# A hybrid encoder block on one core: the order of the last two experts' products on TensorE

## The chip, the cores and the metric

One core of one Trainium2 chip runs the whole block in one launch, in f32. The metric is the device time of a run in microseconds (us), of which the median of several runs counts. Engines are called as in the profile: PE is TensorE (PEld its weight load), DVE is VectorE, ACT is ScalarE, POOL is GpSimd, SP is SyncE, which here only issues transfers.

## What is computed

For 512 tokens of width 1024, one layer:

```
u = RMSNorm(h);  h += concat(pool mixer(u W_in), bidirectional SSM(u W_in)) W_out
v = RMSNorm(h)
every token picks 1 of 4 expert groups and in it 2 of 8 experts (32 experts in all)
h += sum over its two experts of  weight * (silu(v Wg) * (v Wu)) Wd        Wg, Wu: 1024x256, Wd: 256x1024
h += sigmoid(RMSNorm(h) W_g + b_g) * (p W_ple)
out = RMSNorm(h)
```

The change touches the third and fourth line, from the last two experts to the first transposes for the product with `W_g`.

## The kernel before, in words

**Experts.** The tokens of an expert are gathered into 64 places (`CAP`); should an expert have more tokens, overflow rounds run afterwards, inside an `If` on every engine, which is not taken with these inputs. Experts are numbered 0 to 31 (`NE` is 32). For expert e PE runs four steps. `gu_step(e)` is the gate and up product: 16 matmuls of 64 tokens by 256 columns into bank `1 + e % 2`, gate in its lower and up in its upper 64 partitions. ACT's `silu(e)` and DVE's `hidden` turn it into the hidden rows. `h_step(e)` transposes those on PE into bank 3, DVE copies them out, and `down_step(e)` is the down product: 4 matmuls of 512 columns into bank `4 + e % 2`. ACT's `y_out(e)` copies it to the buffer `M_Y + e % 3` and counts `dn_sb` up. For experts 0 to 29 POOL then scatters these rows to a table of pairs (token, first or second expert) in HBM. A matmul of f32 has two records in the trace.

**Order on PE.** The order is written out by hand in the loop over e at line 1988: `h_step(e)`, for some e the transposes of gathered rows (`x_step`), `gu_step(e + 1)`, for some e other small work (`p_rows`, `proj`), and `down_step(e)`. So the next expert's gate and up product covers what ACT and DVE do for this one. ACT has the matching order at line 779: `silu(e + 1)` ahead of `y_out(e)`.

**Weights.** Each expert has three pieces of 1 MB, 96 MB in all, loaded by SP into 22 or so places that are freed by earlier products. SP issues transfers in order, and behind the last piece it issues, each after its wait: the residual `h` back from HBM (2 MB), the first half of half 0 of `W_g` (`load_gate(0, 0, 4)`, 1 MB, when expert 30's gate and up product is done), then `pairs` of token tile 0 (1 MB, when POOL reports `moe_done`, which is after the last scattered rows have been stored, and when expert 30's down product is done), the rest of half 0 (1 MB), then (when expert 31's gate and up product is done) pairs of tile 1, half 1 of `W_g` (2 MB), pairs of tile 2, and pairs of tile 3.

**Combining.** The 512 tokens are 4 tiles (t) of 128. DVE's `combine(t)` first waits for the pairs of tile t, adds the two weighted rows to `h` (4 operations of 512 columns, L1332), and then adds what experts 30 and 31 contribute, which is in PSUM (2 operations, L856, which count the semaphore `comb`). That contribution is not scattered: PE spreads it over the tokens by `combined(t)` at line 1915. For each half n of the columns it has two matmuls, one for expert 30 and one for expert 31, each with a 64 row contraction (n = 0 on the lower 64 rows, n = 1 on the upper ones) into bank `2 * t + n`: 16 spreading products in all. They stand behind `down_step(31)`, the `If`, and a wait for all 32 copies `dn_sb`. Then comes `turned_h(t)` (8 transposes of the new `h` into banks 2t and 2t + 1, each four behind a wait on `comb`), DVE writes the transposed tile to `ut`, and `gate(2 * t)`, `gate(2 * t + 1)` are the products with `W_g` (8 matmuls of 512 columns each). The order is `turned_h(0)`, `gate(0)`, `turned_h(1)`, `gate(1)`, `gate(2)`, and so on:

```
            for t in range(NT):
                combined(t)
            ...
            turned_h(0)
            pe.wait_ge(ld_wple, 32)
            for t in range(NT):
                gate(2 * t)
                if t + 1 < NT:
                    turned_h(t + 1)
                pe.wait_ge(ld_wple1, 16)
                gate(2 * t + 1)
```

PE executes its list in order, so a wait holds up all that stands behind it. All matmuls go through a helper at L1580, whence this line in the profile; L1948 is the transpose of `h_step`, L2044 that of `turned_h`, L754 is `silu`, L531 ACT's copy, L1569 POOL's `moe_done`, L488 and L494 are SP's loads of `W_g` and of the pairs.

## Time and profile before

| | us |
|---|---|
| median of 3 runs | 523.2 (522.0 to 524.99) |
| the profiled execution, its own time | 525.58 |
| its span, first to last instruction | 523.7 |
| PE busy / DVE / ACT / POOL | 482.2 / 239.0 / 163.2 / 159.9 |
| granted PE clock, mean over the span | 0.982 of full speed |
| HBM read / written | 138.17 MB / 16.29 MB |

The profiled execution's own time is 1.9 us above its span; what a step moves is looked for in the span. A row of a timeline gives the start, the length, the engine and line, output and inputs, the count of records, and in brackets the idle time before it with what ended it. In windows the granted clock is a share of full speed (1.00 is 2.4 GHz, 0.50 is 1.2 GHz).

### The profile page before, as it was taken

How to read it: one execution, taken by the hardware profiler on the slowest of the kernel's cores; microseconds unless marked ns; L12 is line 12 of the kernel's file. 1: busy time of each engine (PE TensorE's matmuls, PEld its weight loads, DVE VectorE, ACT ScalarE, POOL GpSimd, SP SyncE). 2: the span in 40 equal slices, each digit the busy share in tenths (PEclk: the TensorE clock that was granted, in tenths of full speed). 3: DMA queues.
4: the chain of work that ended last, by engine and by line, in shares of the span. 5: the costliest groups of instructions: out<-in, count | busy, mean ns of one | idle time of the engine just before them, and what ended most of it. 6: DMA issues, size and time to landing. Idle time of an engine off the chain costs nothing.

```text
span 523.7 us, 7297 instructions
## 1 busy us (share of the span) xinstructions
PE 482.2 (92%) x2744; PEld 271.8 (52%) x2744; DVE 239.0 (46%) x683; ACT 163.2 (31%) x265; POOL 159.9 (31%) x144
## 2 busy tenths in 40 slices
PE   3799999999999998979999999879999998899993
PEld 3446776634844477645555555435454544444441
DVE  2899987999233358632222222202211211474524
ACT  5643335456442344111111111112211121314464
POOL 1069999944100111222222232202120210003350
PEclk9999999999999999979999999989999998999997
DMA  8874200499289966998999999999999997970012
GB/s 295 145 201 88 62 0 2 159 131 212 103 370 419 402 252 259 397 417 334 419 420 417 419 416 414 418 419 421 420 420 418 418 417 299 340 314 0 0 80 80
DMA packets 57083, 146.83 MB, mean 280 GB/s; under 512 B 27602, under 2 KB 32758, under 8 KB 44248
## 3 DMA queue, kind: packets, MB, share of 16 engines
q1 hardware_dynamic: 50872, 133.92, 69.0%
q0 software_dynamic: 5904, 12.41, 6.1%
q8 instruction: 22, 0.36, 0.3%
q14 instruction: 13, 0.11, 0.1%
q10 hardware_dynamic: 272, 0.04, 0.0%
HBM read 138.17 MB, written 16.29 MB: 295 GB/s over the span
## 4 chain that ended last, share of the span: by engine, by line
PE 70%; DMA 20%; ACT 4%; DVE 4%; issue 1%; SPq 0%; DVEq 0%; POOL 0%; POOLq 0%
PE bank L1580 64%; DMA big<-in_exp_w_up_dram 6%; DMA ring<-in_exp_w_up_dram 6%; DMA h<-in_exp_w_up_dram 5%; DMA moe<-v_d,gidx_all 2%; PE bank L1929 2%; DMA h<-in_x_dram 1%; PE bank L1671 1%; ACT moe L531 1%; PE bank L1948 1%; ACT L539 1%; DVE moe L856 1%; PE bank L1815 1%; PE bank L2044 1%; DVE ring L856 1%
## 5 line engine op out<-in xcount | busy, mean ns | idle before, releaser
L1580 PE MATMUL bank<-ring,moe 128*64 128x256 f32 (+3 forms) x976 | 130.1, 392 | 3.8 <-DMA ring<-in_exp_w_up_dram 3.8
L1580 PEld LDWEIGHTS bank<-ring,moe 128*64 128x64 f32 (+1 forms) x976 | 76.9, 147 | 40.7 <-issue 17.4
L1506 POOL DMA_INDIRECT pairs_d<-moe,sidx_all x32 | 31.9, 998 | 163.1 <-PE bank L1929 84.0
L856 DVE TENSOR_TENSOR vrow<-moe,bank 64x128 f32<-64x128 f32 x64 | 18.6, 291 | 125.2 <-ACT moe L754 124.2
L1580 PE MATMUL bank<-ut,big 128*128 128x512 f32 x128 | 57.4, 596 | 2.4 <-ACT ut L543 2.4
L1580 PE MATMUL bank<-big,ut 128*128 128x512 f32 x128 | 56.6, 595 | 1.1 <-ACT ut L676 1.1
L754 ACT ACTIVATE moe<-bank 64x256 f32<-64x256 f32 x32 | 12.1, 377 | 145.9 <-PE bank L1580 145.9
L1580 PE MATMUL bank<-ring,ut 128*128 128x512 f32 x128 | 55.7, 593 | 0.4 <-DVE ut L856 0.4
L531 ACT ACTIVATE moe<-bank 128x512 f32<-128x512 f32 x56 | 32.5, 598 | 62.2 <-PE bank L1580 49.5
L1580 PE MATMUL bank<-big,moe 128*64 128x256 f32 (+1 forms) x264 | 43.5, 443 | 5.3 <-DMA zbuf<-in_exp_w_up_dram 2.5
L856 DVE TENSOR_TENSOR ring<-ring,bank 128x64 f32<-128x64 f32 (+1 forms) x142 | 39.5, 278 | 2.8
L1580 PEld LDWEIGHTS bank<-big,ut 128*128 128x128 f32 x128 | 23.9, 190 | 31.0 <-issue 30.7
L1580 PEld LDWEIGHTS bank<-ring,ut 128*128 128x128 f32 x128 | 24.0, 190 | 29.3 <-issue 29.3
L1580 PEld LDWEIGHTS bank<-ut,big 128*128 128x128 f32 x128 | 23.4, 190 | 27.8 <-issue 27.2
L856 DVE TENSOR_TENSOR bank<-bank,ring 128x64 f32<-128x64 f32 (+1 forms) x142 | 35.2, 287 | 2.9
L1580 PE MATMUL bank<-ring 128*64 128x128 f32 (+1 forms) x128 | 32.5, 437 | 0.0
L1580 PEld LDWEIGHTS bank<-big,moe 128*64 128x64 f32 x264 | 22.0, 142 | 20.1 <-issue 6.4
L1269 DVE COPY moe<-bank 128x128 f32<-128x128 f32 x32 | 9.3, 292 | 45.6 <-PE bank L1948 45.6
L856 DVE TENSOR_TENSOR moe<-bank,vec 128x512 f32<-128x512 f32 x40 | 26.0, 687 | 7.7 <-PE bank L1929 5.7
L1580 PEld LDWEIGHTS bank<-ring 128*64 128x64 f32 (+1 forms) x128 | 15.2, 163 | 15.3 <-issue 15.0
L1574 POOL TENSOR_TENSOR ring<-ring,zbuf 128x512 f32<-128x512 f32 x6 | 8.1, 1350 | 48.3 <-ACT ring L817 48.3
L531 ACT ACTIVATE zbuf<-bank 128x512 f32<-128x512 f32 x16 | 11.5, 717 | 35.9 <-PE bank L1580 35.9
(193 smaller groups left out, 605.0 us busy)
## 6 DMA issues: line engine op xcount, KB each, us to landing
ring<-in_exp_w_up_dram SPq DMA_DIRECT2D x19, 1024.0 KB, 22.8
ring<-in_exp_w_down_dram SPq DMA_DIRECT2D x18, 1024.0 KB, 27.9
ring<-in_exp_w_gate_dram SPq DMA_DIRECT2D x17, 1024.0 KB, 23.3
big<-in_exp_w_gate_dram SPq DMA_DIRECT2D x7, 1024.0 KB, 25.5
big<-in_exp_w_down_dram SPq DMA_DIRECT2D x7, 1024.0 KB, 30.0
big<-in_exp_w_up_dram SPq DMA_DIRECT2D x6, 1024.0 KB, 31.4
ut<-in_exp_w_gate_dram SPq DMA_DIRECT2D x4, 1024.0 KB, 12.8
h<-in_exp_w_up_dram SPq DMA_DIRECT2D x4, 1024.0 KB
```

The costliest lines, as they stand in the source:

```text
L531: act.activation(o, i, ACT.Copy).then_inc(signal, 1)
L539: act.activation(at(small, ALL, S_WARM + k, [[1, 1]]), at(small, ALL, S_EPS, [[1, 1]]), function)
L754: act.activation(at(moe, (0, CAP), M_SG, [[1, DE]]), at(bank[1 + e % 2], (0, CAP), 0, [[1, DE]]), ACT.Silu).then_inc(sg_sb, 1)
L856: return dve.tensor_tensor(o, a, b, op)
L1269: dve.tensor_copy(at(moe, ALL, M_HT + (e % 2) * P, [[1, P]]), bank[3][:, 0:P]).then_inc(hT_sb, 1)
L1506: pool.indirect_dma_start(pairs, bass.IndirectOffsetOnAxis(ap=index, axis=0), at(moe, ALL, M_Y + k * 512, [[1, 512]]), None, bounds_check= ...
L1574: seq(pool.tensor_tensor(sg, sg, at(zbuf, ALL, n * 512, [[1, 512]]), ALU.mult))
L1580: return pe.matmul(o, a, b, start=start, stop=stop, skip_group_check=loose)
L1671: last = pe.transpose(bank[B_WT + ri][:, (g % 4) * P:(g % 4 + 1) * P], rv(R_W + ri * 1024 + g * P, P), ident)
L1815: rows = pe.transpose(bank[H_BANK[t] + n][:, (j % 4) * P:(j % 4 + 1) * P], at(h, ALL, t * DM + j * P, [[1, P]]), ident)
L1929: last = pe.transpose(bank[j // 4 * 6][:, (j % 4) * P:(j % 4 + 1) * P], at(moe, ALL, M_XG + k * DM + j * P, [[1, P]]), ident)
L1948: return pe.transpose(bank[3][:, 0:P], vrow[:, :], ident)
```

## The change

Expert 30's down product is moved ahead of expert 31's gate and up product (and on ACT `y_out(30)` ahead of `silu(31)`). Its eight spreading products are taken out of `combined` and put at several places: tile 0 both halves and tile 3 half 0 behind expert 31's gate and up product, tile 3 half 1 behind expert 31's transpose, tile 1 both halves and tile 2 half 0 behind the `If` and ahead of the wait for expert 31's copy, tile 2 half 1 still inside `combined(2)`. `combined(t)` keeps expert 31's products. `turned_h(0)` now stands between `combined(1)` and `combined(2)`. Overflow rounds, which do not run with these inputs, use banks 2, 5 and 3 in place of 0, 6 and 1, since the spread sums are already standing in the others, and PE waits for all copies ahead of them.

```diff
--- before.py
+++ after.py
@@ -777,7 +777,7 @@
 
             silu(0)
             for e in range(NE):
-                if e + 1 < NE:
+                if e < NE - 2:
                     silu(e + 1)
                 if e == P_ROWS:
                     p_rows_out()
@@ -789,6 +789,8 @@
                 y_out(e)
                 if e == 0:
                     slots_30_out()
+                if e == NE - 2:
+                    silu(e + 1)
             with act.If(most(act) > CAP):
                 act.wait_ge(dn_sb, NE)
                 with act.Fori(1, ROUNDS) as r:
@@ -796,7 +798,7 @@
                         turn = act.snap((r - 1) * NE + e + 1)
                         count = act.snap(turn + NE)
                         act.wait_ge(gu_ps, count)
-                        act.activation(at(moe, (0, CAP), M_SG, [[1, DE]]), at(bank[1], (0, CAP), 0, [[1, DE]]),
+                        act.activation(at(moe, (0, CAP), M_SG, [[1, DE]]), at(bank[3], (0, CAP), 0, [[1, DE]]),
                                        ACT.Silu).then_inc(sg_sb, 1)
                         act.wait_ge(dn_ps, count)
                         copy(at(moe, ALL, M_Y + O_Y * 512, [[1, 512]]), bank[4][:, :], dn_sb)
@@ -1218,12 +1220,12 @@
             peak(qv("r1", [[1, 2 * NT]]), qv("pa", [[NE, 2 * NT], [1, NE]]), ALU.add)
             own.do(dve.tensor_reduce(at(flag, ALL, 0, [[1, 1]]), at(bank[5], ALL, NT * NE, [[1, NE]]), AX.X, ALU.max))
 
-            def x_out(k, signal, rows=0):
+            def x_out(k, signal, rows=0, banks=(0, 6)):
 
                 for n in range(2):
                     if rows:
                         dve.wait_ge(xT_ps, rows - 1 + n)
-                    tt(at(moe, ALL, M_XT + k * DM + n * 512, [[P, 4], [1, P]]), at(bank[n * 6], ALL, 0, [[P, 4], [1, P]]),
+                    tt(at(moe, ALL, M_XT + k * DM + n * 512, [[P, 4], [1, P]]), at(bank[banks[n]], ALL, 0, [[P, 4], [1, P]]),
                        at(vec, ALL, V_FFN + 4 * n, [[1, 4], [0, P]]), ALU.mult).then_inc(signal, 1)
 
             x_out(0, xT_sb, 2)
@@ -1314,9 +1316,9 @@
                         tokens(at(gidx_o, ALL, 0, [[1, 1]]), at(tblw, ALL, e, [[1, 1]]), o_idx)
                         half_rows(at(sidx_o, ALL, 0, [[1, 1]]), at(tblw, ALL, e, [[1, 1]]), o_idx)
                         dve.wait_ge(xT_ps, rows_count)
-                        x_out(0, xT_sb)
+                        x_out(0, xT_sb, 0, (2, 5))
                         dve.wait_ge(sg_sb, count)
-                        hidden(bank[1], hg_sb)
+                        hidden(bank[3], hg_sb)
                         dve.wait_ge(hT_ps, count)
                         dve.tensor_copy(at(moe, ALL, M_HT, [[1, P]]), bank[3][:, 0:P]).then_inc(hT_sb, 1)
             with dve.Else():
@@ -1912,21 +1914,25 @@
                     got = pe.transpose(bank[7 if x == NE - 1 else 6][:, t * P:(t + 1) * P], at(moe, ALL, Q[f"X{x}"] + t * P, [[1, P]]), ident)
                 got.then_inc(ppt_ps, 1)
 
+            def spread(x, t, n):
+
+                parts = (n * CAP, (n + 1) * CAP)
+                turned = (at(ring, parts, E_S + t * P, [[1, P]]) if x == NE - 1 else
+                          at(small, parts, S_S30 + t * P, [[1, P]]) if t < 2 else at(rw, parts, (t - 2) * P, [[1, P]]))
+                return mm(bank[2 * t + n][:, :], turned, at(moe, parts, M_Y + x % YBUF * 512, [[1, 512]]),
+                          x == NE - 2, x == NE - 1, True)
+
             def combined(t):
 
                 for n in range(2):
-                    parts = (n * CAP, (n + 1) * CAP)
-                    for x in (NE - 2, NE - 1):
-                        turned = (at(ring, parts, E_S + t * P, [[1, P]]) if x == NE - 1 else
-                                  at(small, parts, S_S30 + t * P, [[1, P]]) if t < 2 else at(rw, parts, (t - 2) * P, [[1, P]]))
-                        got = mm(bank[2 * t + n][:, :], turned, at(moe, parts, M_Y + x % YBUF * 512, [[1, 512]]),
-                                 x == NE - 2, x == NE - 1, True)
-                    got.then_inc(cmb_ps, 1)
-
-
-            def x_rows(k):
+                    if (t, n) == (2, 1):
+                        spread(NE - 2, t, n)
+                    spread(NE - 1, t, n).then_inc(cmb_ps, 1)
+
+
+            def x_rows(k, banks=(0, 6)):
                 for j in range(KC):
-                    last = pe.transpose(bank[j // 4 * 6][:, (j % 4) * P:(j % 4 + 1) * P],
+                    last = pe.transpose(bank[banks[j // 4]][:, (j % 4) * P:(j % 4 + 1) * P],
                                         at(moe, ALL, M_XG + k * DM + j * P, [[1, P]]), ident)
                     if j % 4 == 3:
                         last.then_inc(xT_ps, 1)
@@ -1985,7 +1991,7 @@
             slots(NE - 2)
             pe.wait_ge(ppt_sb, 2)
             x_step(1)
-            for e in range(1, NE):
+            for e in range(1, NE - 2):
                 h_step(e)
                 if e % 2 == 0 and e + 2 < NE:
                     if e == P_ROWS + 1:
@@ -1993,16 +1999,27 @@
                     if e - 1 in P_PROJ:
                         pe.wait_ge(pp_done, 2 * P_PROJ.index(e - 1) + 2)
                     x_step(e // 2 + 1)
-                if e + 1 < NE:
-                    gu_step(e + 1)
+                gu_step(e + 1)
                 if e == P_ROWS:
                     p_rows()
                 if e in P_PROJ:
                     for n in range(2):
                         proj(e, 2 * P_PROJ.index(e) + n)
                 down_step(e)
+            h_step(NE - 2)
+            down_step(NE - 2)
+            gu_step(NE - 1)
+            pe.wait_ge(ppt_sb, 5)
+            pe.wait_ge(dn_sb, NE - 1)
+            spread(NE - 2, 0, 0)
+            spread(NE - 2, 0, 1)
+            spread(NE - 2, 3, 0)
+            h_step(NE - 1)
+            spread(NE - 2, 3, 1)
+            down_step(NE - 1)
             pe.wait_ge(slot_done, 1)
             with pe.If(most(pe) > CAP):
+                pe.wait_ge(dn_sb, NE)
                 with pe.Fori(1, ROUNDS) as r:
                     with pe.Fori(0, NE) as e:
                         turn = pe.snap((r - 1) * NE + e + 1)
@@ -2012,10 +2029,10 @@
                         dma16 = pe.snap(turn * 16)
                         dma48 = pe.snap(turn * 48)
                         pe.wait_ge(o_xg, dma16)
-                        x_rows(0)
+                        x_rows(0, (2, 5))
                         pe.wait_ge(xT_sb, x_count)
                         pe.wait_ge(o_w, dma48)
-                        gate_up(0, 0, (ring, O_SLOT), (ring, O_SLOT + PIECE), 1).then_inc(gu_ps, 1)
+                        gate_up(0, 0, (ring, O_SLOT), (ring, O_SLOT + PIECE), 3).then_inc(gu_ps, 1)
                         pe.wait_ge(hg_sb, h_count)
                         h_rows().then_inc(hT_ps, 1)
                         pe.wait_ge(hT_sb, count)
@@ -2024,10 +2041,10 @@
             with pe.Else():
                 pass
 
-            pe.wait_ge(ppt_sb, 5)
+            for n in (0, 1):
+                spread(NE - 2, 1, n)
+            spread(NE - 2, 2, 0)
             pe.wait_ge(dn_sb, NE)
-            for t in range(NT):
-                combined(t)
             def gate(n):
                 t, half = n // 2, n % 2
                 for j in range(KC):
@@ -2045,7 +2062,11 @@
                                             at(h, ALL, t * DM + j * P, [[1, P]]), ident)
                     last.then_inc(turned_ps, 1)
 
+            combined(0)
+            combined(1)
             turned_h(0)
+            combined(2)
+            combined(3)
             pe.wait_ge(ld_wple, 32)
             for t in range(NT):
                 gate(2 * t)
```

## Rows read from the trace of the kernel before

**Rows 1.** The page's chain of work that ended last, by engine.

```profile
PE 70%; DMA 20%; ACT 4%; DVE 4%; issue 1%; SPq 0%; DVEq 0%; POOL 0%; POOLq 0%
```

**Rows 2.** The chain in order of time (start us, us, what), the wait for the last weights.

```profile
407.18 31.39 DMA big<-in_exp_w_up_dram
```

**Rows 3.** PE timeline, 430 to 465 us: start us, us, operation [idle before <-releaser].

```profile
430.59 5.39 PE L1580 MATMUL bank<-ring,moe 128*64 128x256 f32 x40 [0.96 <-DMA ring<-in_exp_w_up_dram]
435.92 0.33 PE L1948 MATMUL bank<-cst,vrow 128*128 128x128 f32 x1
438.62 7.08 PE L1580 MATMUL bank<-big,moe 128*64 128x256 f32 x40 [2.38 <-DMA big<-in_exp_w_up_dram]
...
446.34 1.94 PE L1580 MATMUL bank<-big,moe 128*64 128x512 f32 x8 [0.38 <-DVE moe L1269]
449.07 1.14 PE L1580 MATMUL bank<-moe,small 64*128 64x512 f32 x4 [0.79 <-ACT moe L531]
...
456.21 1.09 PE L2044 MATMUL bank<-cst,h 128*128 128x128 f32 x8
457.74 7.11 PE L1580 MATMUL bank<-ring,ut 128*128 128x512 f32 x16 [0.44 <-DVE ut L856]
```

**Rows 4.** Windows around the last expert: busy us per engine, PEclk, DMA share, GB/s.

```profile
436.30:438.62 2.32, 0.00 (x0) 0.00 (x1) 0.27 (x1) 0.33 (x1) 0.98 (x1) 1.00 1.03 407
438.62:446.34 7.72, 7.34 (x41) 3.69 (x41) 0.87 (x3) 0.97 (x2) 0.09 (x1) 0.78 0.48 189
...
449.07:456.21 7.14, 7.14 (x32) 4.00 (x32) 4.21 (x6) 1.82 (x3) 0.00 (x0) 1.00 1.01 399
```

**Rows 5.** Two stretches of 2 us from 228 us on, same columns.

```profile
228.00:230.00 2.00, 0.91 (x5) 0.50 (x7) 1.26 (x4) 0.00 (x0) 1.70 (x2) 0.57 0.99 406
...
232.00:234.00 2.00, 2.00 (x12) 1.13 (x10) 0.00 (x0) 0.00 (x0) 0.00 (x0) 0.50 1.02 422
```

**Rows 6.** PE timeline, 334 to 352 us: two more waits for weights.

```profile
338.34 0.43 PE L1580 MATMUL bank<-big,moe 128*64 128x256 f32 x1 [2.53 <-DMA zbuf<-in_exp_w_up_dram]
...
347.66 4.71 PE L1580 MATMUL bank<-h,moe 128*64 128x256 f32 x26 [3.67 <-DMA h<-in_exp_w_up_dram]
```

**Rows 7.** The 2 us right behind the second of those waits, columns as in Rows 4.

```profile
348.00:350.00 2.00, 2.00 (x12) 1.17 (x10) 0.00 (x0) 0.00 (x0) 0.00 (x0) 0.50 0.97 403
```

**Rows 8.** ACT timeline around the last expert.

```profile
444.03 0.38 ACT L754 ACTIVATE moe<-bank 64x256 f32<-64x256 f32 x1 [7.40 <-PE bank L1580]
...
448.33 0.60 ACT L531 ACTIVATE moe<-bank 128x512 f32<-128x512 f32 x1 [1.99 <-PE bank L1580]
```

**Rows 9.** DVE timeline, 444 to 458 us.

```profile
444.44 0.61 DVE L856 TENSOR_TENSOR vrow<-moe,bank 64x128 f32<-64x128 f32 x2 [7.87 <-ACT moe L754]
...
451.46 2.99 DVE L1332 SCALAR_TENSOR_TENSOR h<-big,small,h 128x512 f32<-128x512 f32 x4 [5.17 <-DMA big<-pairs_d]
454.55 1.29 DVE L856 TENSOR_TENSOR h<-bank,h 128x512 f32<-128x512 f32 x2
456.90 1.29 DVE L856 TENSOR_TENSOR ut<-bank,vec 128x512 f32<-128x512 f32 x2 [1.07 <-PE bank L2044]
```

**Rows 10.** POOL timeline: the step behind the last stored rows.

```profile
444.23 0.09 POOL L1569 MEMSET fill<- 1x1 int32 x1 [5.85 <-issue]
```

**Rows 11.** SP timeline: issues of the gate weights' first half and of the pairs.

```profile
434.31 0.38 SPq L488 DMA_DIRECT2D ring<-in_ple_gate_w_dram  x1
445.79 0.34 SPq L494 DMA_DIRECT2D big<-pairs_d  x1
446.17 0.43 SPq L488 DMA_DIRECT2D ring<-in_ple_gate_w_dram  x1
```

**Rows 12.** DMA issues of 434 to 435 us: the last column is us to landing.

```profile
ring<-in_ple_gate_w_dram SPq DMA_DIRECT2D x1, 1024.0 KB, 14.6
```

**Rows 13.** DMA issues of 446.1 to 446.3 us and the one before them, us to landing.

```profile
big<-pairs_d SPq DMA_DIRECT2D x1, 1024.0 KB, 5.6
ring<-in_ple_gate_w_dram SPq DMA_DIRECT2D x1, 1024.0 KB, 8.5
```

## The prediction

> **What bounds the kernel now.** I read the chain first: PE holds 70% of the span, DMA 20% [rows 1]. In order of time, PE has to wait for the up weights of expert 31, which land at 438.6 [rows 2], and from there every piece up to the tail is PE's: the change lies on the path that sets the end. The reader should then walk PE's timeline from 435.9 us on [rows 3]: the transpose of expert 30, an idle 2.38 us for the weights, 7.08 us for 40 records (32 of expert 31's gate and up product, 8 of expert 30's down product), an idle 0.38, 1.94 for expert 31's down product, an idle 0.79, the spreading products from 449.07, the first transposes of the new h at 456.21, an idle 0.44, and from 457.74 the products with W_g, which run on to the tail. These four idle times, 4.0 us together, are what the change can fill. The start of gate(0), 457.74, is the point to watch: all behind it is untouched and stays PE's, so the time moves by what this start moves.
>
> Next look at who else arrives at that point. DVE begins tile 0 at 451.46, as the pairs of tile 0 land, after 5.17 us of waiting; four operations take 2.99, and the two that add the spread sums 1.29, from 454.55 to 455.84 [rows 9]. PE comes to the transposes only 0.4 us later, at 456.21 [rows 3]. So PE and the chain DMA, DVE, PE are nearly level at this point, and shortening one of them alone gives little. That is the main reading.
>
> **What ends the wait for the pairs.** SP issues them at 445.79 [rows 11], right after expert 30's down product, and they land 5.6 us later, at 451.4 [rows 13]. Ahead of them in SP's list stands 1 MB of W_g, issued at 434.31 [rows 11] and landing 14.6 us later, at 448.9 [rows 12]. Behind them stands the next 1 MB, issued at 446.17 and landing 8.5 us later, at 454.7 [rows 11, 13]. Landings 2.5 and 3.3 us apart fit transfers of 1 MB passing one after the other: at the 399 GB/s of the busy stretch 1 MB takes 2.6 us [rows 4]. Yet between 438.62 and 446.34 the mean DMA share is only 0.48 [rows 4]: most of the 16 engines have finished, and the slowest still work on the earlier pieces. I conclude that a landing is set by the slowest engine, which has a backlog until 448.9, and that pairs issued at any time before that land at 451.4. The Trainium skill (DMA: Bandwidth & Descriptors, Queues, rings and completion order) says that each engine takes its descriptors in the order of its ring; by that rule too a short new transfer waits behind the backlog, and the spacing above agrees.
>
> **The change, part by part.**
>
> 1. Expert 30's down product moves into the wait for the weights. Its weights stand ahead of expert 31's in SP's list. The transpose ends at 436.25, DVE's copy takes as long as the same step at expert 31, where PE idled 0.38, and the product takes 1.94 [rows 3]: 436.6 to 438.5, so it fits before 438.6. It no longer stands behind the gate and up product: 8 records, a good 1.7 us (1.94 less the last one's tail), are off PE.
>
> 2. With this wait filled, the clock should not fall there. Between 438.62 and 446.34 it was 0.78 of full speed on the mean, after 2.32 us without a matmul [rows 4]. At full clock such 40 records take 5.4 us (the same mixture starting at 430.59 did [rows 3]), so the fall cost 7.08 - 5.4 = 1.7.
>
> 3. What used to be hidden behind expert 30's down product now has no such cover: silu begins as the gate and up product ends and takes 0.38, DVE's two operations 0.61 with 0.03 between [rows 8, 9]; with hand-overs 1.35 us from the end of the product to the next transpose. Three spreading products take the cover's place. 16 of them take 7.14 us, 0.45 each, with two on different halves of the rows side by side [rows 4]; a lone one takes up to twice that. So tile 0's two take 0.9 and tile 3's one 0.45 to 0.9: 1.7 us for 1.35 of cover. Another lone one, up to 0.9, stands ahead of expert 31's down product for an idle 0.38; three more, 1.7, stand where 0.79 was idle [rows 3]. The If's register load may show there: 0 to 0.79, since all of it lay inside that idle time before.
>
> 4. The sum on PE. Gate and up 438.6 to 442.3 (32 records of the full-clock rate, 3.7), spreads to 444.0, transpose 0.3, spread to 445.2, down product to 446.9, three spreads to 448.6, expert 31's on tile 0 and tile 1, two times 0.86, to 450.3. Before, PE had all 16 done at 456.2. Six microseconds early, it now stands at `turned_h(0)`.
>
> 5. Other queues. ACT copies expert 30's rows at 438.5, ahead of silu(31), which is not due until 442.3: free. On SP the pairs no longer wait for the down product but for POOL's report at 444.23 [rows 10], so they and all behind them are issued some 1.5 us earlier. By the reading above that changes no landing. No transfer is added, and DVE's list is the same.
>
> 6. `turned_h(0)` needs DVE's two sums, and these need the pairs: 451.46 + 2.99 + 0.1 + 1.29 = 455.84 as before. PE idles from 450.3 to 455.2 for the first half, 4.9 us, and is through both halves at about 456.3 (4 transposes behind 455.84). Before, all spreading was over here. Now five products still stand between the transposes and gate(0): 31 on tile 2 twice, 30 on tile 2 half 1, 31 on tile 3 twice. At 0.45 each they take 2.25, in three steps of 0.86 they take 2.6; I take 2.6 because their halves pair only in part. gate(0) starts at 458.9 against 457.74: **1.2 us later**. Every gain of 1 to 3 is spent in the 4.9 us wait.
>
> 7. The clock again. The new wait is twice the one that made it fall at the end before. In this trace, waits of 2.38 and 3.67 us were followed by half clock [rows 3, 4, 6, 7], one of 2.53 was not [rows 6]; a 4.9 us wait I expect to be followed by it. The price: nothing (as after 2.53), 1.7 us as worked out in 2, or more: between 228 and 234 us the clock was at half for at least 5.7 us (a mean of 0.57 in the first 2 us means 1.7 us at 0.50, and from 232 to 234 it is still 0.50 [rows 5]), half of which, 2.9, is lost. Here part of the low stretch falls into waiting for DVE. I take 2.1, between 1.7 and 2.9. The Trainium skill (TensorE: Matmul & The Clock Gate, HAM oscillation) warns of just this: a wait for DMA between groups of matmuls lets the clock drop, and the next group starts slowly. The trace agrees in three waits of four.
>
> Sum against the profiled execution: +1.2 + 2.1 = +3.3 on the span of 523.7, that is 527.0, and 528.9 for its own time of 525.58. The median shown, 523.2, lies 2.4 below that execution; I add the same 3.3 to it: **526.5 us**. Should the median's runs not have had the fall at 438, the difference to them grows by up to 1.
>
> **Rivals.**
>
> A. The pairs land as much earlier as they are issued, 1.5 us, at 449.9. For it: the engines are half idle at 446 [rows 4]. Against it: the spacing of landings. Then the sums are ready at 454.35, PE is free to spread at 454.9, and gate(0) starts at 457.5: 0.2 earlier; with 0 to 1.7 for the clock 523.0 to 524.7. This is the one on the other side, not slower: it decides if the pairs land by 450.3, where the later start of gate(0) is cancelled. The Trainium skill (same DMA page, Latency and other measured facts, and the anatomy ahead of it) puts a transfer's fixed cost near 2 us; by that figure the pairs, issued at 444.3, would land about as this rival says.
>
> B. The wait is there, but the clock doesn't fall behind it, or only inside the wait: +1.2, 524.4, not to be told from no change.
>
> C. The clock stays low for two stretches or the baseline runs had no fall at 438: +4 to +5, 527.2 to 528.2.
>
> D. The change doesn't do what it says: expert 30's down product doesn't fit before 438.6. Even a full 1.9 us late it would be swallowed by the wait at `turned_h(0)`: same result as the forecast.
>
> **How the numbers follow.** Forecast with D 0.50, C 0.13, A 0.17, B 0.15, and 0.05 for a gain that I see no way to. A measurement of this kernel tells about 0.5%, 2.6 us, from no change. The forecast's own range is 525.2 to 527.7 and the bound lies at 525.8, so some 0.45 of its 0.50 is slower, with all of C: 0.57. A, B and the rest of the forecast are within 0.5%: 0.38. Faster gets 0.05. The range reaches down to A's 523.0 with the clock staying up and up to C's 528.3.
>
> **What would show it.** In the trace after: 8 records of 64 columns by 512 between 436.6 and 438.6, and 1.00 as clock behind them; the pairs of tile 0 issued near 444.3 and landing near 451.4 (A: near 450); an idle PE for 4 to 5 us ahead of L2044's first transposes, ended by DVE's L856; half clock behind it; gate(0) starting at 459 to 461. I am wrong if that idle time is under 2 us, if the clock stays at 1.00 through it, or if gate(0) starts before 457.7.

## The result and the profile after

Over 6 runs each, in turns on one chip, the changed kernel has a median of 528.3 us and the kernel before 523.1, 5.2 us apart. The ratio that the comparison gives, which is not the quotient of the medians, is 1.0086, with a 95% interval of 1.0062 to 1.0110: slower by 0.9%, 4.5 us (3.2 to 5.8 by the interval). A second comparison, run with the experiments, gave 1.0064 (1.0030 to 1.0099), 3.4 us; three of its 12 runs of the change, far out at 539 to 2836 us, are in neither its ratio nor its median. Forecast were 526.5 against 523.2 (+3.3) and a range up to 528.3. The direction comes out, but the median lies at the very end of the range, above the forecast's own 525.2 to 527.7. By size the first comparison agrees with rival C (+4 to +5), the second with the forecast.

The profiled execution after took 525.65 us, the fastest of its six runs and the one with the highest mean clock (0.988; the others have 0.969 to 0.984), and its span is 523.7, the same as the span before. So the two spans must not be compared; the stretch around the change can be. The page's chain gives PE 71% and, which it did not have before, 1% each for the pairs and for the stored rows ahead of them:

```profile
PE 71%; DMA 19%; DVE 4%; ACT 4%; issue 1%; SPq 1%; POOLq 0%; DVEq 0%; POOL 0%
PE bank L1582 65%; DMA ring<-in_exp_w_up_dram 12%; DMA big<-in_exp_w_up_dram 4%; PE bank L1935 2%; DMA h<-in_x_dram 1%; PE bank L1673 1%; DMA big<-pairs_d 1%; DMA pairs_d<-moe,sidx_all 1%; PE bank L1954 1%; PE bank L2061 1%; ACT moe L531 1%
```

PE's timeline after, from expert 30's gate and up product on (the helper is now L1582, the transpose of the hidden rows L1954, `turned_h` L2061); it answers to [rows 3]:

```profile
427.74 5.39 PE L1582 MATMUL bank<-ring,moe 128*64 128x256 f32 x40 [1.48 <-DMA ring<-in_exp_w_up_dram]
433.06 0.33 PE L1954 MATMUL bank<-cst,vrow 128*128 128x128 f32 x1
433.77 5.50 PE L1582 MATMUL bank<-big,moe 128*64 128x512 f32 x40 [0.38 <-DVE moe L1271]
439.20 1.13 PE L1582 MATMUL bank<-moe,small 64*128 64x512 f32 x4
...
441.12 0.33 PE L1954 MATMUL bank<-cst,vrow 128*128 128x128 f32 x1
...
442.43 1.94 PE L1582 MATMUL bank<-big,moe 128*64 128x512 f32 x8
444.30 1.13 PE L1582 MATMUL bank<-moe,small 64*128 64x512 f32 x4
...
445.80 2.20 PE L1582 MATMUL bank<-moe,ring 64*128 64x512 f32 x7
452.38 1.72 PE L2061 MATMUL bank<-cst,h 128*128 128x128 f32 x8 [4.39 <-DVE h L858]
...
455.89 1.99 PE L1582 MATMUL bank<-moe,ring 64*128 64x512 f32 x6
457.81 7.13 PE L1582 MATMUL bank<-ring,ut 128*128 128x512 f32 x16
```

Of idle time ahead of the last products only 0.38 us is left: expert 30's down product and expert 31's gate and up product now form one piece of 40 records, and from 433.77 to 448.00 PE is busy without a break. Then comes one wait of 4.39 us, ended by DVE's sum, where none was. Before, PE took 25.6 us from the start of expert 30's gate and up product to the transposes (430.59 to 456.21, [rows 3]); now 24.6. From there to the first product with W_g it was 1.5 us and is 5.4.

DVE's timeline after says why PE waits [rows 9]:

```profile
448.54 2.99 DVE L1334 SCALAR_TENSOR_TENSOR h<-big,small,h 128x512 f32<-128x512 f32 x4 [6.76 <-DMA big<-pairs_d]
451.63 1.29 DVE L858 TENSOR_TENSOR h<-bank,h 128x512 f32<-128x512 f32 x2
```

Counted from the same event, the start of expert 30's gate and up product, DVE begins on the pairs at 448.54 - 427.74 = 20.80 us, against 451.46 - 430.59 = 20.87 before. SP's timeline and the issue's own row show that they were issued earlier, 13.8 us after that event in place of 15.2, and took 6.9 us in place of 5.6 to land [rows 11, 13]:

```profile
441.57 0.34 SPq L494 DMA_DIRECT2D big<-pairs_d  x1
```

```profile
big<-pairs_d SPq DMA_DIRECT2D x1, 1024.0 KB, 6.9
```

Windows of the wait and of what follows it, up to the first product with W_g (columns as in [rows 4]); the first fence is the changed kernel, the second the same kernel in the second comparison:

```profile
448.00:452.38 4.38, 0.00 (x1) 0.00 (x1) 3.67 (x6) 0.00 (x0) 0.00 (x0) 1.00 1.03 413
452.38:457.81 5.43, 5.43 (x18) 2.70 (x18) 4.81 (x8) 1.45 (x3) 0.00 (x0) 0.69 1.06 401
```

```profile
448.10:452.51 4.41, 0.00 (x1) 0.01 (x1) 3.67 (x6) 0.00 (x0) 0.00 (x0) 0.91 1.03 411
452.51:459.21 6.70, 6.70 (x18) 3.42 (x18) 5.72 (x10) 1.45 (x3) 0.00 (x0) 0.55 1.05 406
```

The wait is the same, 4.4 us, and both times half clock follows it; the same 8 transposes and 5 spreading products then take 5.4 us in one execution and 6.7 in the other. A mean of 0.69 over 5.43 us means 3.4 us at half clock; in the second execution the two windows together have 6.8 us of it, twice as much.

### The profile page after: what moved, and what is told of

Its sections match the earlier page's. It is cut to its first block, busy times and chain, and to the rows that moved or that the text cites. A ratio compares the mean times of both kernels' runs of the same rounds, so it can differ in the third digit from the quotient of the medians.

```text
span 523.7 us, 7297 instructions
## 1 busy us (share of the span) xinstructions
PE 482.8 (92%) x2744; PEld 270.5 (52%) x2744; DVE 239.0 (46%) x683; ACT 163.2 (31%) x265; POOL 159.8 (31%) x144
## 4 chain that ended last, share of the span: by engine, by line
PE 71%; DMA 19%; DVE 4%; ACT 4%; issue 1%; SPq 1%; POOLq 0%; DVEq 0%; POOL 0%
PE bank L1582 65%; DMA ring<-in_exp_w_up_dram 12%; DMA big<-in_exp_w_up_dram 4%; PE bank L1935 2%; DMA h<-in_x_dram 1%; PE bank L1673 1%; DMA big<-pairs_d 1%; DMA pairs_d<-moe,sidx_all 1%; PE bank L1954 1%; PE bank L2061 1%; ACT moe L531 1%; ACT L539 1%; DVE moe L858 1%; PE bank L1817 1%; DVE ring L858 1%
## 5 line engine op out<-in xcount | busy, mean ns | idle before, releaser
L1582 PE MATMUL bank<-ring,moe 128*64 128x256 f32 (+3 forms) x976 | 128.8, 388 | 4.8 <-DMA ring<-in_exp_w_up_dram 4.8
L1582 PEld LDWEIGHTS bank<-ring,moe 128*64 128x64 f32 (+1 forms) x976 | 76.3, 145 | 40.8 <-issue 16.0
L858 DVE TENSOR_TENSOR vrow<-moe,bank 64x128 f32<-64x128 f32 x64 | 18.6, 291 | 121.7 <-ACT moe L754 120.7
L1582 PE MATMUL bank<-ut,big 128*128 128x512 f32 x128 | 57.4, 596 | 2.6 <-ACT ut L543 2.6
L1582 PE MATMUL bank<-big,ut 128*128 128x512 f32 x128 | 56.6, 595 | 1.1 <-ACT ut L676 1.1
L1582 PE MATMUL bank<-ring,ut 128*128 128x512 f32 x128 | 55.7, 593 | 0.0
L1582 PE MATMUL bank<-big,moe 128*64 128x256 f32 (+1 forms) x264 | 43.6, 436 | 3.8 <-DMA zbuf<-in_exp_w_up_dram 2.9
L1582 PEld LDWEIGHTS bank<-big,ut 128*128 128x128 f32 x128 | 23.9, 190 | 31.0 <-issue 30.7
L1582 PEld LDWEIGHTS bank<-ring,ut 128*128 128x128 f32 x128 | 24.0, 190 | 29.5 <-issue 29.5
L1582 PEld LDWEIGHTS bank<-ut,big 128*128 128x128 f32 x128 | 23.4, 190 | 27.9 <-issue 27.4
L1582 PE MATMUL bank<-ring 128*64 128x128 f32 (+1 forms) x128 | 32.5, 437 | 0.0
L1582 PEld LDWEIGHTS bank<-big,moe 128*64 128x64 f32 x264 | 21.9, 139 | 19.8 <-issue 6.4
L1582 PEld LDWEIGHTS bank<-ring 128*64 128x64 f32 (+1 forms) x128 | 15.2, 163 | 15.3 <-issue 15.0
```

The costliest lines, as they stand in the source:

```text
L858: return dve.tensor_tensor(o, a, b, op)
L1582: return pe.matmul(o, a, b, start=start, stop=stop, skip_group_check=loose)
```

## The experiments

Since the spans differ for reasons further up (waits for expert weights and half clock stretches that no edit here touches), I read each trace first by one distance that lies wholly in the stretch of the change: from DVE's first operation on the pairs of tile 0 to PE's first product with W_g. Before it is 457.74 - 451.46 = 6.3 us [rows 3, 9], after 9.3, and in the second trace of the change 10.5. It can't show an earlier landing of the pairs, since it starts there. So the last column has a second distance, which holds all that a kernel pays from the change on: from the start of expert 30's gate and up product to the end of the span. Before it is 523.7 - 430.59 = 93.1 us, with the change 96.0. What lies behind the change is the same in all of them, as the prediction had it: from the first product with W_g to the end it is 65.9 to 66.0 us in every trace but four (66.1 in e5 and e10, 67.5 in e9, 68.1 in e2).

Times are compared by their ratios to the kernel before, whose runs alternate with each kernel's. There are three comparisons: e1 to e4, e5 to e8, and e9 to e11. e2 to e4 were not run beside the change, so they are set against it by two ratios, 1.0086 and 1.0064. How far a ratio strays by itself is seen in e8, the kernel before against itself: 0.9983. In expectations, idle times and clock are those ahead of and behind `turned_h(0)`.

| run | median | before | ratio, 95% interval | distance | to the end |
|---|---|---|---|---|---|
| e1 down product alone | 523.2 | 523.7 | 0.9993 (0.9966 to 1.0020) | 5.4 | 92.0 |
| e11 the same again | 522.3 | 523.6 | 0.9992 (0.9969 to 1.0015) | 5.4 | 92.1 |
| e2 change, all spreading ahead | 524.7 | 523.7 | 1.0022 (0.9999 to 1.0044) | 5.8, then slow | 94.9 |
| e3 change, wait filled | 525.4 | 523.7 | 1.0042 (1.0012 to 1.0073) | 7.8 | 94.6 |
| e4 change, pairs first | 523.7 | 523.7 | 1.0017 (0.9991 to 1.0042) | 7.8 | 92.3 |
| e5 e2 and e4 together | 522.8 | 524.2 | 0.9985 (0.9956 to 1.0014) | 6.6 | 91.6 |
| e10 the same again | 522.8 | 523.6 | 0.9981 (0.9962 to 1.0001) | 6.8 | 91.5 |
| e6 before, pairs first | 524.5 | 524.2 | 0.9992 (0.9966 to 1.0019) | 7.2 | 92.9 |
| e7 the change again | 527.6 | 524.2 | 1.0064 (1.0030 to 1.0099) | 10.5 | 97.5 |
| e8 before again | 523.2 | 524.2 | 0.9983 (0.9952 to 1.0015) | 6.1 | 93.2 |
| e9 e5, second half of W_g later | 522.3 | 523.6 | 0.9979 (0.9960 to 0.9998) | 5.4 | 91.6 |

**e1 and e11: the down product alone.** All of the change undone but the order of expert 30's down and expert 31's gate and up product; `combined(t)` has both experts' products again:

```diff
             gu_step(NE - 1)
-            pe.wait_ge(ppt_sb, 5)
-            pe.wait_ge(dn_sb, NE - 1)
-            spread(NE - 2, 0, 0)
...
             h_step(NE - 1)
-            spread(NE - 2, 3, 1)
             down_step(NE - 1)
...
-            combined(0)
-            combined(1)
+            for t in range(NT):
+                combined(t)
             turned_h(0)
-            combined(2)
-            combined(3)
```

> Expert 30's down product ahead of expert 31's gate and up product, and nothing else: all 16 spreading products together ahead of the first transposes, as before. My theory (the arrival of the pairs of tile 0 sets the first transposes, and what matters is what PE still has to do behind them): the spreading products end near the time at which DVE's sums are ready, no idle time over 1 us ahead of the transposes, clock 1.00, and the products with W_g start 0.5 to 1.2 us earlier than before relative to the landing of the last up weights. Time 0 to 1.5 us below before, 4 to 6 below the change. Rival (the moved down product is itself what costs): as slow as the change, +4 to +5 against before.

> e1 once more: only expert 30's down product moved. My theory: 0.5 to 1 us below before, which is what its trace showed between the pairs' landing and the products with W_g (5.4 against 6.1 to 6.3), clock 1.00 behind the wait for expert 31's weights. Rival (no difference): within 0.3 us of before.

PE's timeline of e1:

```profile
442.90 0.33 PE L1953 MATMUL bank<-cst,vrow 128*128 128x128 f32 x1 [1.12 <-DVE vrow L858]
...
446.34 1.14 PE L1582 MATMUL bank<-moe,small 64*128 64x512 f32 x4 [0.79 <-ACT moe L531]
...
454.88 1.25 PE L2052 MATMUL bank<-cst,h 128*128 128x128 f32 x8 [1.33 <-DVE h L858]
456.42 7.10 PE L1582 MATMUL bank<-ring,ut 128*128 128x512 f32 x16 [0.28 <-DVE ut L858]
```

With none of the later waits filled, PE is still at the transposes 1.3 us too early, more than the 1 us expected. The distance is 0.7 to 0.9 us shorter than in the two traces of before. The time is not below before by anything that can be told (0.9993 and 0.9992), though 0.9 us would be only 0.17%; e11's rival, no difference, stands. What falls is the rival that the moved down product costs 4 to 5 us.

**e2: all spreading ahead of the transposes.**

```diff
-            combined(0)
-            combined(1)
+            for t in range(NT):
+                combined(t)
             turned_h(0)
-            combined(2)
-            combined(3)
```

> The change with one edit: all spreading products of tiles 2 and 3 stand ahead of the first transposes again. My theory: the idle time at the transposes shrinks from 4.4 to about 2.2 us, the five products (2.2 to 2.6 us) are off the path behind it, and the products with W_g start 2.2 us earlier than with the change at the same clock, 3 to 4 earlier if the clock does not fall. Time 2.2 to 4 us below the change, within 1.5 us of before. Rival (the wait for the pairs and the clock behind it are all that counts, the five products are hidden): no more than 0.5 us below the change.

```profile
453.49 1.97 PE L2061 MATMUL bank<-cst,h 128*128 128x128 f32 x8 [2.56 <-DVE h L858]
455.48 9.31 PE L1582 MATMUL bank<-ring,ut 128*128 128x512 f32 x16
```

The ratio is 0.64% below the first one of the change, 3.4 us, in the middle of what was expected, and 0.42% below the second, 2.2 us, at its lower end. The wait shrank to 2.56 us, but half clock came all the same: the product with W_g took 9.31 us in place of 7.13 and the transposes 1.97 in place of 1.25, 2.9 us more. So this trace still pays for the clock, and no longer for the five products.

**e3: the wait filled.**

```diff
             combined(1)
+            for k in range(10):
+                spread(NE - 2, 3, k % 2)
             turned_h(0)
```

> The change with ten more spreading products of expert 30 for tile 3 in PE's wait ahead of the first transposes (each restarts the same sum, 4.5 us of work in a wait of 4.4 to 4.9). My theory: the clock stays at 1.00 there, the transposes begin at most 0.3 us later, and the 1.7 us of the half clock stretch come back: time 1 to 2 us below the change, still 2 to 3 above before because of the five products behind the transposes. Rival (the low clock is not what the wait costs, or more work only delays): same as the change, or 1 us and more above it.

```profile
447.71 4.77 PE L1582 MATMUL bank<-moe,rw 64*128 64x512 f32 x19
452.54 1.25 PE L2061 MATMUL bank<-cst,h 128*128 128x128 f32 x8
```

```profile
447.70:452.50 4.80, 4.78 (x22) 2.22 (x18) 3.62 (x6) 0.00 (x0) 0.00 (x0) 1.00 1.02 406
452.54:456.50 3.96, 3.96 (x19) 1.90 (x19) 3.63 (x7) 1.45 (x3) 0.00 (x0) 1.00 1.08 400
```

Ten more matmuls that are of no use make the traced stretch shorter: with no wait left, the clock stays at 1.00 and the transposes and five products take 4.0 us in place of 5.4 and 6.7. That is the clock's price, 1.5 and 2.7 us. It is one trace, but the runs point the same way: the mean clock of e3's 11 is 0.984, that of the 15 of the change 0.979. The ratio, 1.0042, lies 2.3 us below the first one of the change and 1.2 below the second, and its interval overlaps with both, so by the times alone the gain is not clear. The other part is still there: a distance of 7.8 against 6.3, and a ratio above 1 by its whole interval.

**e4: the pairs ahead of the first load of W_g.**

```diff
             sp.wait_ge(gu_ps, NE - 1)
-            load_gate(0, 0, 4, ld_wple)
             sp.wait_ge(moe_done, 1)
             sp.wait_ge(dn_ps, NE - 1)
             load_pairs(0)
+            load_gate(0, 0, 4, ld_wple)
             load_gate(0, 4, 4, ld_wple)
```

> The change with SP's load of the first 1 MB of W_g moved behind the pairs of tile 0 (same bytes, other order). My theory (a landing is set by the backlog of the slowest DMA engine, in order): the pairs land 2.5 us earlier, 1 MB at about 400 GB/s, the first transposes begin 2.5 us earlier, the idle time ahead of them is about 2 us, and the time is 2 to 3.5 us below the change. The gate weights land where they did and do not become the bound. Rival (a landing comes a fixed time after its issue, 5.6 to 7 us): the pairs land as in the change, to 0.5 us, and the time is the same.

```profile
437.54 3.67 PE L1581 MATMUL bank<-big,moe 128*64 128x256 f32 x32 [0.27 <-DMA big<-in_exp_w_up_dram]
...
451.69 1.25 PE L2060 MATMUL bank<-cst,h 128*128 128x128 f32 x8 [1.75 <-DVE h L857]
...
455.64 7.13 PE L1581 MATMUL bank<-ring,ut 128*128 128x512 f32 x16
```

```profile
447.85 2.99 DVE L1333 SCALAR_TENSOR_TENSOR h<-big,small,h 128x512 f32<-128x512 f32 x4 [4.13 <-DMA big<-pairs_d]
```

From the last up weights to DVE's start it is now 447.85 - 437.54 = 10.3 us; it was 12.8 before (451.46 - 438.62) and 12.9 in e8. Counted from the start of expert 30's gate and up product it is 18.6, against 20.8 and 21.0 in the two traces of the change. So the pairs come 2.3 to 2.5 us earlier when 1 MB ahead of them is taken away, while issuing them 1.4 us earlier, which is what the change did, brought next to nothing: in the six traces with the 1 MB ahead in which they are issued at 13.7 to 14.0 us, DVE starts at 20.8 to 21.0, and in the two of the old order, issued at 15.2 and 15.3, at 20.9 and 21.2. The ratio of 1.0017 is 3.6 us below the first one of the change and 2.5 below the second: this one edit on SP takes back most of the loss. The traces have 2.3 us for the landing and 1.5 to 2.7 for the clock, which stays at 1.00 behind a wait of 1.75 us. Together that is 3.8 against the first trace of the change and 5.0 against the second; nothing of it is given back behind the first product with W_g, from which it is 66.0 us to the end here too.

**e5 and e10: both edits.** The diffs of e2 and e4 together.

> The change with both edits: all spreading products ahead of the first transposes, and the pairs of tile 0 ahead of the first 1 MB of W_g. My theory: PE's spreading ends 22.2 us and DVE's sums are ready 22.7 us after the start of expert 30's gate and up product; under 1 us of idle time, clock 1.00, the products with W_g start at 24 to 24.5 (before 27.15 with its slow stretch, with the change 30.07), bounded then by the landing of W_g's first 2 MB at 24.1. Time 1 to 3 us below before, 6 to 8 below the change. Rival (the gains at this point are taken back behind it, by the pairs of the later tiles or the tail): same as before to 0.5 us.

> e5 once more, beside e9 and e11, since its time was not clear of the kernel before. My theory: 1 to 2.5 us below before (as its trace has it: the products with W_g start earlier, with a wait of 1.5 us for 2 MB of W_g ahead of them), clock 1.00 from expert 30 to the tail. Rival: same as before within 0.5 us.

e5's timeline of PE:

```profile
451.58 1.26 PE L2060 MATMUL bank<-cst,h 128*128 128x128 f32 x8 [0.69 <-DVE h L857]
454.33 5.85 PE L1581 MATMUL bank<-ring,ut 128*128 128x512 f32 x13 [1.50 <-DMA ring<-in_ple_gate_w_dram]
```

PE and DVE meet within 0.7 us (0.2 in e10), the clock stays up there, and then PE waits 1.5 us for W_g (1.7 in e10). The second MB of it was issued at 443.6 and landed 10.7 us later, at 454.3: 25.5 us after the start of expert 30's gate and up product, where I had put 24.1, as before, and where the changed kernel has 23.4. Windows show what most of it can come from, the stretch from about the last up weights to the issue of the pairs in e5, and the same of the changed kernel:

```profile
436.50:442.75 6.25, 6.25 (x42) 3.31 (x41) 0.78 (x3) 0.98 (x2) 0.23 (x2) 1.00 0.35 142
```

```profile
435.60:441.57 5.97, 5.97 (x42) 3.22 (x41) 0.67 (x3) 0.97 (x2) 0.09 (x1) 1.00 0.60 238
```

With W_g's first MB moved behind the pairs, the engines that are done with the experts have nothing to do: 142 GB/s in place of 238, over 6 us some 0.6 MB, or 1.5 us at 400 GB/s, out of the 2.1 by which W_g comes later than in the changed kernel. 0.9985 and 0.9981 lean to faster by 0.8 to 1.0 us, at or below the lower end of the expectations, and neither interval excludes no change; nor do they differ from the 0.9983 that the kernel before gave against itself in e8. Against the change, in the same comparison as e5, they do: 1.0064 (from 1.0030) against 0.9985 (to 1.0014), 4.1 us.

**e6 and e8: the kernel before with e4's edit, and the kernel before again.**

> The kernel before with the pairs of tile 0 ahead of the first 1 MB of W_g, nothing else. My theory: the pairs land 2.5 us earlier, but the kernel before has its spreading products ahead of the transposes and PE is the later one there, so that the products with W_g start 0 to 1 us earlier and the time is within 1 us of before. Rival (the landing of the pairs bounds the kernel before too): 2 us and more below before.

> The kernel before once more, unchanged, for a second trace of it. My theory: the products with W_g start 26.0 to 27.2 us after the start of expert 30's gate and up product, 26.0 to 26.5 if the clock does not fall behind the wait for expert 31's weights, the pairs landing at 20.8. Time the same as before. Rival (the start varies by more than that from run to run): outside this.

In e6 the time did not move (0.9992), as the theory has it for a kernel where PE is the later one: DVE's sums were ready at 456.7 and PE came to the transposes at 458.0, without any wait. But the pairs did not gain the 2.5 us there: SP could issue them only behind expert 30's down product, at 447.53, and they landed 4.8 us later; DVE's start lies 12.0 us behind the last up weights in place of 12.8, a gain of 0.9 where 2.5 were expected. Beside e4's it shows something else. First e4, then e6, the issue and the time from it to the landing:

```profile
443.07 0.33 SPq L494 DMA_DIRECT2D big<-pairs_d  x1
big<-pairs_d SPq DMA_DIRECT2D x1, 1024.0 KB, 4.8
```

```profile
447.53 0.33 SPq L494 DMA_DIRECT2D big<-pairs_d  x1
big<-pairs_d SPq DMA_DIRECT2D x1, 1024.0 KB, 4.8
```

The pairs are issued 13.8 us after the start of expert 30's gate and up product in e4 and 15.0 in e6, and take 4.8 us both times (4.8 to 5.0 in e5, e9 and e10). So once the 1 MB of W_g is out of their way, a landing does follow its issue at a fixed time. The backlog's rule holds only as long as there is a backlog, and that e4 gained close to the 2.5 us of 1 MB is in part luck: what it could gain was bounded by its issue.

In e8, as in the first trace, the wait for expert 31's weights is followed by half clock:

```profile
433.44:436.09 2.65, 0.00 (x1) 0.00 (x1) 0.29 (x1) 0.38 (x1) 0.98 (x1) 0.96 1.01 399
436.09:443.30 7.21, 7.20 (x41) 3.62 (x41) 0.58 (x2) 0.59 (x2) 0.09 (x1) 0.78 0.55 218
```

It is in e6's trace too: its 40 records behind 2.17 us of waiting took 7.08 us. So all three traces of the old order pay 1.6 to 1.7 us there, and the sum's base was the ordinary case as far as three traces tell. e8's first product with W_g starts at 27.3 us, where 26.0 to 27.2 was expected, and its pairs are at 21.2 in place of 20.8.

**e7: the change again.**

> The changed kernel once more, unchanged, beside e5, e6 and e8 on one chip. My theory: 2.5 to 5 us above before; in the trace the pairs land 20.8 us after the start of expert 30's gate and up product, PE idles 4 to 5 us ahead of the transposes, a stretch of half clock follows, the products with W_g start at 29.5 to 31.5. Rival (the first comparison was a matter of the chip or of its runs): within 1 us of before.

1.0064 lies within the expectation, and its trace has been shown above: pairs at 21.0, 4.4 us of waiting, half clock, the first product with W_g at 459.21 - 427.69 = 31.5, at the upper end of the expectation.

**e9: the second half of W_g later.** e5 and:

```diff
             load_gate(0, 0, 4, ld_wple)
-            load_gate(0, 4, 4, ld_wple)
             sp.wait_ge(gu_ps, NE)
             load_pairs(1)
+            load_gate(0, 4, 4, ld_wple2)
...
-            pe.wait_ge(ld_wple, 32)
+            pe.wait_ge(ld_wple, 16)
...
                 for j in range(KC):
+                    if n == 0 and j == 4:
+                        pe.wait_ge(ld_wple2, 16)
```

> e5 and one step more: SP loads the pairs of tile 1 ahead of the second 1 MB of W_g, and PE waits for that second 1 MB only inside the first product with W_g, under a semaphore of its own. My theory (in e5 the first product with W_g waited 1.5 us for 2 MB, and behind it the pairs of tile 1 were nearly level): that product starts right behind the transposes, waits 0.3 to 1 us in its middle, and ends 0.5 to 1.2 us earlier than in e5. Time 0.5 to 1.2 us below e5, 1 to 3 below before. Rival (the order of the landings only moves the wait): same as e5.

```profile
451.35 1.21 PE L2063 MATMUL bank<-cst,h 128*128 128x128 f32 x8
452.88 3.67 PE L1582 MATMUL bank<-ring,ut 128*128 128x512 f32 x8 [0.32 <-DVE ut L858]
456.80 3.70 PE L1582 MATMUL bank<-ring,ut 128*128 128x512 f32 x8 [0.25 <-DMA ring<-in_ple_gate_w_dram]
460.34 1.04 PE L2063 MATMUL bank<-cst,h 128*128 128x128 f32 x8
462.22 7.99 PE L1582 MATMUL bank<-ring,ut 128*128 128x512 f32 x18 [0.84 <-DMA ring<-in_ple_gate_w_dram]
```

The wait of 1.5 us ahead of the product is now 0.25 in its middle, but 0.84 us for half 1 of W_g came up behind the next transposes. The first product with W_g ends 1.0 us earlier than in e5's trace (460.34 against 461.30, both with expert 30's gate and up product starting at 428.85), but the next one starts at 462.22 against 462.24, and both spans are 520.4 us. So the expected gain over e5 did not come, and the rival holds: the other order only moved the wait. Against e10 the median is 0.46 us lower, less than the two can be told apart. It is the only version whose interval lies below the kernel before, 0.9979 (0.9960 to 0.9998), but the kernel before gave 0.9983 against itself, so a gain of 1 us over it is not shown for any version. By the two ratios of the change it lies 4 to 6 us below that.

## Why the prediction was right, step by step

**The main reading** held: PE and the chain of DMA and DVE were nearly level at the transposes, so PE's saving turned into a wait. PE came there with 4.4 us in hand where I had worked out 4.9.

**Step 1 and 2**, the down product in the wait for weights and the clock behind it: as forecast. From 433.77 to 448.00 the clock is 1.00 and PE has no idle time. Alone (e1, e11) this part shortens the distance by 0.7 to 0.9 us, and in the time it can't be told from nothing.

**Step 3**, what the waits were filled with: the same to 0.6 us. The If's register load, bounded by 0 and 0.79, showed as nothing: the products behind it begin at 444.30, before the down product's last record has ended (442.43 + 1.94).

**Step 5**, the other queues: the pairs went out at 441.57 just behind POOL's report at 441.45, and landed where the backlog put them, 20.8 us after expert 30's start. Rival A, a fixed time after the issue, is out for the change: 5.6 us from issue to landing became 6.9, and only taking bytes away ahead of them (e4) moved the landing. Behind such an edit it comes true: 4.8 to 5.0 us in five traces, at two times of issue. The Trainium skill's figure for a transfer's fixed cost, near 2 us (DMA: Bandwidth & Descriptors, Latency and other measured facts) does not set the landing in the change; in those five traces it is close to it, since 4.8 less the 2.6 us of the 1 MB leaves 2.2. Its statement on the order within a ring (Queues, rings and completion order) agrees with the rows of the change. That it is the slowest of the 16 engines which holds the landing back was argued from the DMA share of 0.48 [rows 4]; no run looked at a single engine.

**Step 6**, five products behind the transposes, 1.2 us: mis-sized by 0.3 to 0.5. At full clock (e3, e4) the distance is 7.8 against 6.1 to 6.3 before, +1.5 to 1.7. In e4 the five products take 455.64 - 452.87 = 2.8 us, where I had 2.6, since their halves pair only in part.

**Step 7**, the clock, 2.1 us between 1.7 and 2.9: two traces show 1.5 and 2.7, and e3, in which the wait is filled, shows the cause. Rival B, no fall of the clock, is out: the two traces of the change and the one of e2 all show it. The count of "three waits of four" is a loose one: the third fall, at 228 us, stands behind waits of 1.04 and 1.59 us for ACT and DVE, so of the waits for DMA it was two of three.

The sum of 3.3 stands against 3.0 and 4.3 in the two traces, and 4.5 and 3.4 us by the two ratios. The profiled execution, 525.65 us, was the mildest of six, so it understates the loss. Whether the rest is a longer half clock stretch in the median run, as in e7's trace, is not shown, since the other runs have no trace; their mean clocks, 0.969 to 0.984 against its 0.988, point that way.

**Rival C**, a low clock for two stretches and +4 to +5, is what e7's trace shows: 6.8 us of half clock in place of 3.4, and the first product with W_g 4.4 us later than before from the common event. So the mechanism of the forecast is right, but which of the two stretches an execution gets decides between its size and rival C's, and that the median of 528.3 still lies in a range that ends there owes something to luck. The other half of C, a baseline without the fall at 438 us, is in none of the three traces of before.

**The signs of being wrong**, taken word for word, were partly met in the first trace: the clock is 1.00 all through the wait (448.00 to 452.38) and falls right behind it, and the first product with W_g starts at 457.81, 0.1 us above the bound of 457.7, because this execution reached expert 30 2.9 us earlier. Counted from expert 30 it starts 30.07 us on, against 27.15 before.

**Rival D** needs no more than PE's timeline after: the down product fits.

## What to carry to other kernels

Before filling an engine's waits, ask who else arrives at the next meeting point, and when: if another chain is level with it, the work saved comes back as one long wait, and what then counts is what ends that wait and what stands behind it, so put nothing there that could stand ahead. Issuing a transfer earlier is of use only if the queue ahead of it is empty (4.8 us to landing whenever the pairs were first); with a backlog, change the order or take bytes away. Idle time that is "free" can be paid for behind it: the one long wait of the change was followed by half clock in both of its traces, and the same stretch with the wait filled was not. And compare a kernel with itself before believing a gain of 0.2%.

## What I had not expected of the hardware

Waits as short as 2.2 to 2.7 us were followed by half clock in all three traces of the old order, and in e2 one of 2.56 us brought as much of it as 4.4 us did in e7: 453.49 to 464.63 ran at 0.71 on the mean, against 1.00 in e1 behind 1.33 us of waiting.

```profile
453.49:464.63 11.14, 11.12 (x25) 5.47 (x26) 6.20 (x10) 2.89 (x6) 0.00 (x0) 0.71 1.03 406
```

So a wait's price is not in proportion to its length: 2.56 us cost 2.9 in that trace, 4.4 us cost 1.5 and 2.7, and 1.75 us (e4) nothing. Nor does the length decide whether there is a price. In the trace of before the half clock stretch of [rows 5], at least 5.7 us long, stands behind two waits which are both shorter than e4's:

```profile
226.41 1.09 PE L1929 MATMUL bank<-cst,moe 128*128 128x128 f32 x8 [1.04 <-ACT rw L531]
229.09 0.48 PE L1948 MATMUL bank<-cst,vrow 128*128 128x128 f32 x1 [1.59 <-DVE vrow L856]
```

And in e3 a wait of 3.06 us for weights, up to 361.2, was followed by full clock. What decides it these traces do not show.

The idle share of the transfer engines was worth something after all. Between the last up weights and the pairs only 0.6 of them are busy in the changed kernel, and none of that work is waited for next; yet when e5 took it away from there, W_g landed 1.4 us later than worked out and PE waited 1.5 us for it: what fills the idle engines is work that has to be done anyway.
